# Middle of the mixer in a hybrid encoder layer: meta rows in four column groups, fewer and wider cumulative-sum products among the value products, one activation table set

## What is computed

```python
log_a = log_sigmoid(a1 @ gla_w_a2 + gla_b_a) / TAU          # GLA decay
cum = cumsum(log_a over the chunk); total = cum[last]
k_dec = k * exp(total - cum); u = k_dec^T v; S = exp(total) * S + u; o = q S
dt = softplus(dt_raw + bias); cum = cumsum(dt * a over the chunk)   # SSD, the same form
w = exp(total - cum) * dt; u = B^T (w * xs); h = exp(total) * h + u; y = C h
mix = concat(rms_norm(o) * silu(og), rms_norm((y + d * xs) * silu(z)))
h = layer_norm(alpha * h + mix @ w_out)
h = layer_norm(alpha * h + sum over the 4 experts of gate * (clamped_swiglu(h Wg, h Wu) Wd))
```

## Time and profile before

| | before |
|---|---|
| median of 3 runs | 1094.92 us (1094.44 to 1095.21) |
| the profiled execution | 1093.93 us, of which the span of instructions is 1091.9 us |
| PE busy | 1029.9 us (94%), mean granted clock 0.993 |
| DVE, ACT, POOL busy | 227.2, 145.7, 25.4 us |
| moved by DMA | 426.54 MB, 391 GB/s over the span |
| mixer, to the first expert product | 0 to 176.5 us |

### The profile page before, as it was taken

How to read it: one execution, slowest core, us unless ns; L and a number is a source line. 1 busy time by engine, 2 the same in 40 slices (tenths; PEclk the granted TensorE clock), 3 DMA queues, 4 the chain that set the end, 5 groups by cost and what they waited for, 6 DMA issues and landing times.

```text
span 1091.9 us, 12309 instructions
## 1 busy us (share of the span) xinstructions
PE 1029.9 (94%) x5060; PEld 452.4 (41%) x5060; DVE 227.2 (21%) x496; ACT 145.7 (13%) x345; POOL 25.4 (2%) x47
## 2 busy tenths in 40 slices
PE   9999999999999999999999999999999999999995
PEld 8887745434333443333333333333333333333331
DVE  5422464111111111111111111111111111111114
ACT  2241413111111111111100111111001111101100
POOL 1230100000000000000000000000000000000000
PEclk9989999999999999999999999999999999999998
DMA  9894449999999999999999999999999999999994
GB/s 321 269 349 155 133 161 384 409 431 426 428 427 428 427 428 429 428 428 429 429 428 427 429 429 429 428 427 430 429 428 429 428 429 428 427 429 427 429 427 170
DMA packets 51471, 426.54 MB, mean 391 GB/s; under 512 B 8058, under 2 KB 24547, under 8 KB 26483
## 3 DMA queue, kind: packets, MB, share of 16 engines
q1 hardware_dynamic: 48738, 423.78, 93.4%
q10 hardware_dynamic: 2704, 2.36, 0.8%
HBM read 425.08 MB, written 1.05 MB: 390 GB/s over the span
## 4 chain that ended last, share of the span: by engine, by line
PE 56%; DMA 41%; DVE 2%; ACT 1%; issue 0%; POOL 0%; DVEq 0%; SPq 0%; POOLq 0%
DMA ring<-in_moe_w_up 22%; PE bank L1066 20%; DMA ring<-in_moe_w_gate 18%; PE bank L1105 12%; PE bank L1046 3%; PE bank L1038 3%; PE bank L747 3%; PE bank L944 3%; PE bank L933 1%; PE bank L887 1%; PE bank L703 1%; PE bank L823 1%; PE bank L1094 1%; PE bank L1057 1%; PE bank L763 1%; PE bank L849 1%
## 5 line engine op out<-in xcount | busy, mean ns | idle before, releaser
L1066 PE MATMUL bank<-ring,arena 128*64 128x512 f32 x2000 | 449.0, 595 | 43.9 <-DMA ring<-in_moe_w_up 33.2
L1066 PEld LDWEIGHTS bank<-ring,arena 128*64 128x64 f32 x2000 | 138.1, 136 | 323.9 <-issue 237.9
L1105 PE MATMUL bank<-ring,arena 128*64 128x512 f32 x1024 | 226.8, 595 | 0.7 <-issue 0.7
L1105 PEld LDWEIGHTS bank<-ring,arena 128*64 128x64 f32 x1024 | 71.1, 137 | 151.9 <-issue 151.9
L1470 DVE COPY arena<-bank 128x512 f32<-128x512 f32 x32 | 22.1, 692 | 324.5 <-PE bank L1105 324.5
L656 ACT ACTIVATE arena<-arena 128x512 f32<-128x512 f32 x32 | 20.1, 630 | 457.6 <-DVE arena L1457 457.6
L1046 PE MATMUL bank<-arena 64*128 64x512 f32 x256 | 72.0, 640 | 0.9 <-DVE arena L1470 0.9
L1038 PEld LDWEIGHTS bank<-arena 128*128 128x128 f32 x480 | 58.8, 196 | 22.8 <-issue 22.8
L1463 DVE TENSOR_SCALAR arena<-bank 128x512 f32<-128x512 f32 x32 | 22.1, 691 | 217.8 <-PE bank L1066 217.8
L667 ACT ACTIVATE arena<-bank 128x512 f32<-128x512 f32 x32 | 19.1, 597 | 343.0 <-PE bank L1094 343.0
L1038 PE MATMUL bank<-arena 128*128 128x128 f32 x480 | 64.5, 288 | 0.0
(11 more groups left out here) (271 smaller groups left out, 499.9 us busy)
## 6 DMA issues: line engine op xcount, KB each, us to landing
ring<-in_moe_w_down SPq DMA_DIRECT2D x64, 2048.0 KB, 35.4
ring<-in_moe_w_up SPq DMA_DIRECT2D x63, 2048.0 KB, 34.8
ring<-in_moe_w_gate SPq DMA_DIRECT2D x62, 2048.0 KB, 31.9
ring<-in_w_in SPq DMA_DIRECT2D x12, 1024.0 KB, 12.8
ring<-in_w_out SPq DMA_DIRECT2D x4, 1024.0 KB, 12.2
arena<-in_moe_w_gate SPq DMA_DIRECT2D x4, 1024.0 KB, 7.1
arena<-in_moe_w_up SPq DMA_DIRECT2D x2, 1024.0 KB, 9.1
arena<-in_x SPq DMA_DIRECT2D x2, 512.0 KB, 4.7
```

The source lines that it names most:

```text
L1066: ins = mm(b[h * SL:(h + 1) * SL, :], (xA[pp], xB)[q][:, k, par * SL:(par + 1) * SL], unit_at(UPM * m + q, k)[:, h * 512:(h + 1) * 512], s ...
L1105: ins = mm(bank[6][h * SL:(h + 1) * SL, :], hidT[:, kt % 4, (kt // 4) * SL:(kt // 4 + 1) * SL], unit_at(2 * UPM + q, k)[:, h * 512:(h + 1) ...
```

## The change

`MH` gets four groups of 16 partitions (0, 32, 64, 96) in place of two. Each meta product is cut to half the moving columns and twice the count: keys 64 columns, values 128, logits 64. ACT and DVE handle the four groups as one instruction over 112 partitions, in place of two instructions. In the GLA update of the meta chunk each head now stands on its own row group, with a `link` before each head but the first.

The sums: `dt_m` is `dt_c` masked into four chunk columns by `ind` (a 128x2 indicator of the two halves), made by one more DVE instruction, so that one product with `ones` gives all SSD totals; the triangle product takes both token halves at once. The GLA totals take `la` as the stationary operand of 128 rows and `ind` as two moving columns. Two links go. The keys' second half moves behind the logits, the SSD sums stand between the two halves of the first value products, and the meta triangle products stand each behind a quarter of the second value products; `D_ps` is signalled after the last of these. Products of odd and even chunks alternate in `ssd_update` and `ssd_out`.

On ACT the set `natural_log_exp_and_others` is loaded ahead of the softplus and again behind the Sigmoid of z. The transposes of the SSD half move before the last quarter of the og products, and their copies between the two Sigmoids of og, into a tile `mixY` of its own.

```diff
...
-MH = (slice(0, META), slice(64, 64 + META))
-MH1 = 64 + META
+MH = tuple(slice(32 * g, 32 * g + META) for g in range(4))
+MH1 = 96 + META
 SR = 64 + GRANK + SHEADS
-HK, HV = GKEY // 2, GVAL // 2
+HK, HV = GKEY // 4, GVAL // 4
 RING = 8
...
         la = cut(10368, NT, GKEY)
-        expD = cut(10880, GKEY // 2, parts=MH1)
+        expD = cut(10880, HK, parts=MH1)
         qT = cut(11136, 2, SEQ)
         cacc = cut(11648, 2, TOK)
...
+            nc.scalar.preload_act_table_set("natural_log_exp_and_others")
...
             tmpf = tmp[:, :, :].rearrange("p t n -> p (t n)")
             link(nc.scalar.activation(tmpf, bank[2][:, :], ACT.Abs))
-            for m in MH:
-                link(nc.scalar.activation(expD[m, :], bank[0][m, 0:HK], ACT.Abs))
+            mh = slice(0, MH1)
+            link(nc.scalar.activation(expD[mh, :], bank[0][mh, 0:HK], ACT.Abs))
             link(nc.scalar.activation(tmpf, tmpf, ACT.Exp, scale=-1.0))
-            for m in MH:
-                link(nc.scalar.activation(expD[m, :], expD[m, :], ACT.Exp, scale=-1.0))
+            link(nc.scalar.activation(expD[mh, :], expD[mh, :], ACT.Exp, scale=-1.0))
             link(nc.scalar.activation(tmpf, tmpf, ACT.Ln, bias=1.0))
-            for m in MH:
-                ins = nc.scalar.activation(expD[m, :], expD[m, :], ACT.Ln, bias=1.0)
-            ins.then_inc(la_sp, 1)
+            nc.scalar.activation(expD[mh, :], expD[mh, :], ACT.Ln, bias=1.0).then_inc(la_sp, 1)
             act.wait_ge(dsum_ps, 1)
...
                 nc.scalar.activation(z_t[:, t, :], bank[(0, 5)[t]][:, :], ACT.Sigmoid).then_inc(z_sig, 1)
...
+            act.wait_ge(mixT_ps, 1)
+            mixT_evac(bank[0], mixY, 0)
+            act.wait_ge(mixT_ps, 2)
+            mixT_evac(bank[5], mixY, 2)
             og_sigmoid(1)
-            act.wait_ge(mixT_ps, 1)
-            mixT_evac(bank[0], 4)
-            act.wait_ge(mixT_ps, 2)
-            mixT_evac(bank[5], 6)
             act.wait_ge(mixT_ps, 3)
-            mixT_evac(bank[6], 0)
...
-            def token_major(outs, n):
-
-                for t in range(NT):
-                    for kt in range(KT):
-                        ins = mm(outs[t], hT[:, kt, META + t * P:META + (t + 1) * P], wslot(n, kt), start=kt == 0, stop=kt == KT - 1)
+            def token_major(out, n, t):
+
+                for kt in range(KT):
+                    ins = mm(out, hT[:, kt, META + t * P:META + (t + 1) * P], wslot(n, kt), start=kt == 0, stop=kt == KT - 1)
                 return ins
             def meta_rows(dst, cols, slots):
...
-            token_major([bank[4][:, t * 256:(t + 1) * 256] for t in range(NT)], U_K)
-            meta_rows(bank[1][:, 256:256 + HK], HK, ((U_K, 0), (U_K, HK))).then_inc(k_ps, 1)
+            token_major(bank[4][:, 0:256], U_K, 0)
+            meta_rows(bank[1][:, 64:64 + HK], HK, [(U_K, g * HK) for g in range(4)])
             pe.wait_ge(sT_ok, 1)
             for dst, a, m in ((bank[1][:, 0:8], META, P), (bank[1][:, 8:16], META + P, P), (bank[1][0:META, 16:24], 0, META)):
                 ins = mm(bank[0][m, 0:HK], sT[:, 0:META], w_a2e[:, g * HK:(g + 1) * HK], start=True, stop=True)
             ins.then_inc(la_ps, 1)
+            token_major(bank[4][:, 256:512], U_K, 1).then_inc(k_ps, 1)
+
             pe.wait_ge(w_landed[U_V], 16)
             pe.wait_ge(conv, 8)
             pe.wait_ge(cT_ok, 6)
-            token_major([bank[5][:, 0:256], bank[7][:, 0:256]], U_V)
+            token_major(bank[5][:, 0:256], U_V, 0)
             pe.wait_ge(dt_ok, 1)
-            for t in range(NT):
-                mm(bank[6][:, t * 8:(t + 1) * 8], tri[:, :], dt_c[:, t, :], start=True, stop=True)
+            mm(bank[6][:, 0:16], tri[:, :], dt_c[:, 0:NT, :], start=True, stop=True)
             mm(bank[6][0:META, 16:24], tri[0:META, 0:META], dt_c[0:META, 2, :], start=True, stop=True)
-            for c in (0, 2, 1, 3):
-                r = CHUNK * (c % 2)
-                if c == 1:
-                    link(ins)
-                ins = mm(bank[6][:, 32 + c * 8:40 + c * 8], ones[r:r + CHUNK, :], dt_c[r:r + CHUNK, c // 2, :], start=True, stop=True)
-            ins.then_inc(dsum_ps, 1)
-
+            mm(bank[6][:, 32:64], ones[:, :], dt_m[:, :, :], start=True, stop=True).then_inc(dsum_ps, 1)
+
+            token_major(bank[7][:, 0:256], U_V, 1)
             pe.wait_ge(la_ok, 1)
             for t in range(NT):
                 mm(bank[2][:, t * 256:(t + 1) * 256], tri[:, :], la[:, t, :], start=True, stop=True)
-            mm(bank[0][MH[0], 0:HK], tri[MH[0], MH[0]], la_m[MH[0], :], start=True, stop=True)
-            for c in (0, 2, 1, 3):
-                r = CHUNK * (c % 2)
-                if c == 1:
-                    link(ins)
-                    mm(bank[0][MH[1], 0:HK], tri[MH[1], MH[1]], la_m[MH[1], :], start=True, stop=True)
+            for t in range(NT):
                 for i in range(2):
-                    ins = mm(bank[0][:, GKEY + i * 4 + c:GKEY + i * 4 + c + 1], la[r:r + CHUNK, c // 2, i * P:(i + 1) * P],
-                             ones[r:r + CHUNK, 0:1], start=True, stop=True)
-            ins.then_inc(D_ps, 1)
+                    at = GKEY + i * 4 + 2 * t
+                    mm(bank[0][:, at:at + 2], la[:, t, i * P:(i + 1) * P], ind, start=True, stop=True)
             pe.wait_ge(w_landed[U_V + 1], 16)
-            n = U_V + 1
-            for dst, at in ((bank[5], META), (bank[7], META + P)):
-                for kt in range(KT):
-                    ins = mm(dst[:, 256:512], hT[:, kt, at:at + P], wslot(n, kt), start=kt == 0, stop=kt == KT - 1)
-                ins.then_inc(v_ps, 1)
-            meta_rows(bank[3][:, 0:HV], HV, ((U_V, 0), (U_V + 1, 0))).then_inc(v_ps, 1)
+            for n, (m, dst, at) in enumerate(zip(MH, (bank[5], bank[5], bank[7], bank[7]), (META, META, META + P, META + P))):
+                for kt in range(4 * (n % 2), 4 * (n % 2) + 4):
+                    ins = mm(dst[:, 256:512], hT[:, kt, at:at + P], wslot(U_V + 1, kt), start=kt == 0, stop=kt == KT - 1)
+                if n % 2:
+                    ins.then_inc(v_ps, 1)
+                ins = mm(bank[0][m, 0:HK], tri[m, m], la_m[m, :], start=True, stop=True)
+                if n == 3:
+                    ins.then_inc(D_ps, 1)
+            meta_rows(bank[3][:, 0:HV], HV, [(U_V + g // 2, (g % 2) * HV) for g in range(4)]).then_inc(v_ps, 1)
             pe.wait_ge(wx_ok, 1)
             ssd_banks = (1, 6, 4, 1, 6)
-            def ssd_update(c):
-                b = bank[ssd_banks[c]]
-                for g in range(SGRP):
-                    if c == 0:
-                        k, w = Bt[0:META, 2, g * SST:(g + 1) * SST], xs[0:META, 2, g * 256:(g + 1) * 256]
-                    else:
-                        r = CHUNK * ((c - 1) % 2)
-                        k, w = Bt[r:r + CHUNK, (c - 1) // 2, g * SST:(g + 1) * SST], xs[r:r + CHUNK, (c - 1) // 2, g * 256:(g + 1) * 256]
-                    ins = mm(b[:, g * 256:(g + 1) * 256], k, w, start=True, stop=True)
-                ins.then_inc(us_ps, 1)
+            def ssd_update(c, g):
+                if c == 0:
+                    k, w = Bt[0:META, 2, g * SST:(g + 1) * SST], xs[0:META, 2, g * 256:(g + 1) * 256]
+                else:
+                    r = CHUNK * ((c - 1) % 2)
+                    k, w = Bt[r:r + CHUNK, (c - 1) // 2, g * SST:(g + 1) * SST], xs[r:r + CHUNK, (c - 1) // 2, g * 256:(g + 1) * 256]
+                ins = mm(bank[ssd_banks[c]][:, g * 256:(g + 1) * 256], k, w, start=True, stop=True)
+                if g:
+                    ins.then_inc(us_ps, 1)
             pe.wait_ge(kdec, 1)
-            for c in range(3):
-                ssd_update(c)
+            for g in range(SGRP):
+                ssd_update(0, g)
+            for g in range(SGRP):
+                for c in (1, 2):
+                    ssd_update(c, g)
             pe.wait_ge(w_landed[U_Q], 16)
             pe.wait_ge(v_ok, 1)
             def gla_update(c):
...
+                    if c == 0 and h:
                         link(ins)
                     dst = b[64 * (h % 2):64 * (h % 2) + 64, at + (h // 2) * GDV:at + (h // 2 + 1) * GDV]
                     if c == 0:
-                        m, i = MH[h // 2], h % 2
-                        kk, vv = k_m[m, i * GDK:(i + 1) * GDK], v_m[m, i * GDV:(i + 1) * GDV]
+                        kk, vv = k_m[MH[h], :], v_m[MH[h], :]
                     else:
                         r = CHUNK * ((c - 1) % 2)
                         kk, vv = k_t[r:r + CHUNK, (c - 1) // 2, h * GDK:(h + 1) * GDK], v_t[r:r + CHUNK, (c - 1) // 2, h * GDV:(h + 1) * GDV]
...
                 ins = gla_update(c)
             ins.then_inc(ug_ps, 1)
-            for c in (3, 4):
-                pe.wait_ge(Ss_ok, c - 2 + 0)
-                ssd_update(c)
+            pe.wait_ge(Ss_ok, 2)
+            for g in range(SGRP):
+                for c in (3, 4):
+                    ssd_update(c, g)
             pe.wait_ge(q_ok, 1)
...
-            def ssd_out(c):
```

(36 more changed lines are left out.)

41 lines of the change are left out of this document (21 added, 20 removed).

## The result

The changed kernel takes 1086.32 us (median of 4 runs, 1085.14 to 1087.47), the kernel before 1094.79 (1094.44 to 1095.21). The prediction was wrong in its size; its mechanism held.

The account below looks back on a forecast made before the run. PE's work before the last mixer product sets, one to one, when the saturated weight stream starts. Terms -1.1 - 2.2 - 1.4 - 1.7 + 0 + 0.3 + 0.1 + 1.0 - 0.9 = -5.9 us gave 1089.0, range 1087.0 to 1092.4.

Parts of the forecast that it names:

- Rival D: Stream start: PE time is saved but the stream starts no earlier, loads already issued filling it; 1094.9 us, chance 0.04.
- C: Rival: clock still falls once, at the sums or between meta keys and time steps; costs 3.3, 1092.3 us, chance 0.10.
- E: Rival: clock falls at meta keys with time steps, marked totals and GLA meta update; 3.3 each, 1098.9 us, chance 0.04.
- links: GLA meta update: three links in place of one, two more times 0.5, so 1.0 us worse; the one certain loss.
- alternation: SSD updates and outputs: chunks already run in pairs, so alternating their order gains 0, to 0.3 us better.
- F: Rival: products keep their order on PE, so alternation pairs chunks in SSD updates and outputs; 2.6 us gained, 1086.4, chance 0.05.
- Meta keys: Meta key products on PE: 64 instructions at 29 ns take 1.86 us again, no gain; ends 0.9 better, 1.5 worse.
- B's worst case: Rival: four column groups run no faster than two; with 52 ns for both meta products 1092.0 us; rival's chance 0.15.
- GLA sums: GLA sums on PE: 4.42 us become 2.2, triangles 1.06 and eight two-column products 1.1; gain 2.2 us.
- Second value products: Second value products on PE: 9.77 us become 8.4, 7.1 at full clock plus four meta triangles at 0.32; gain 1.4.
- if a load stayed, 7 us would cover it: ACT's tables before the SSD sums: two wide halves on PE, 7 us, would hide a remaining table load of 1.28 us.
- The change of the chain to the stream: Profile sign: the chain that ended last changes from PE to the stream's transfers at about 393 us, before at 399.

Follow-up runs that it names:

- the pair: The changed kernel with one link in the GLA meta update and the four meta triangles together behind the marked totals: 1083.69 us, ratio 0.9904.
- all three: The changed kernel with one link in the GLA meta update, meta triangles together and GpSimd's long products behind the logarithms: 1083.84 us, ratio 0.9908.

## Why the prediction was wrong in size and right in kind

Right, by its own steps:
- PE's order of work sets the start of the stream, one to one: 7.86 us earlier on PE, 7.8 of span, and 6.4 to 7.0 for 7.1 added in the mixer. Rival D is out.
- No clock fall at the sums (1.00 from 68 to 78), nor there in any other profile with the new sums, so the 3.3 us came back, and C is out. E named a real danger: of its three places the GLA meta update does see falls, in three profiles of kernels with the new sums (transposes put back, GpSimd later, triangles together). That the profiled execution of the changed kernel has none was luck in part.
- Meta values 1.88 (forecast 1.86), links +0.95 (+1.0), transposes -1.05 (-0.9, shown by their undoing), alternation 0 (shown), SSD sums 0.70 (0.8). F is out, although its number, 1086.4, is nearly the one measured: that is chance, since its 2.6 us of pairing are not there.

The step that failed is the size of several terms of PE's sum, 1.9 us in all; the largest is the one for the meta keys, put at nothing:
- Meta keys, the largest: 0 forecast, -0.84 measured. I took 29 ns for one instruction as a floor, since no row showed less. No row showed four column groups with so few columns either. They passed at 16 ns, and at 9 ns with 32 columns. With B's worst case, 52 ns, this was doubt in the wrong direction.
- GLA sums: -2.2 forecast, -2.75 measured. The eight products of two columns on 128 rows took 0.81 us in place of 1.1, and the triangle ahead of them 0.86 in place of 1.06. Both now stand between full-height products, where in before a 16-row product followed; two profiles fit with that. Where products of 64 rows followed (the kernel with old sums) the triangle took 0.96, and where 16-row products followed (triangles together) the eight took 0.88. The range gave all the sums 0.2 us of room, and they came 0.7 better.
- Second value products: -1.4 forecast, -1.25 measured. One spread triangle costs 0.35 (8.52 less 7.11, divided by 4). The form used there was close, but four together cost 0.23 in all: so 1.2 of the 1.4 us is the price of the spreading. That this part of the change loses time against the simple order was nowhere in the forecast; I had set it beside the old 9.77 alone.
- Small ones: SSD sums -0.14, cut halves -0.17 (0.13 for three restarts, not 0.3), wait ahead of the SSD updates -0.1, transposes -0.15, logits -0.1.

A further 0.7 us of the miss in the median comes from the starting point: the profiled execution of before lay 1.0 under its median, that of after 0.3, in runs that scatter by 2.3. This took the time out of the range: with PE's 7.85 us alone it would be 1094.92 - 7.85 = 1087.07, just inside. The range counted only the prices of PE's work and left no room for executions that differ by more than 2 us.

A reason that fell though its number held: "if a load stayed, 7 us would cover it". The tables did bring nothing that the rows show, but the 7 us were not there. The chain of the time steps ended 0.06 us before PE came, held by GpSimd's products, and in executions in which the clock rose earlier at the start (at 5.35 and 6.2 us in place of 8.34) PE waited there 1.17 and 0.38 us (the kernel with chunk order put back, and the changed kernel's second profile). The same holds in all six profiles with GpSimd's products in their place in which the clock rose by 6.2 us: PE waits 0.38 to 1.30 us, and in those with a later rise no wait shows. I had read DVE's durations from an execution in which GpSimd was done, and moved them to a place where it isn't.

The change of the chain to the stream was forecast at about 393 us. It came at 440 in the profile. The chain of before has its next such transfer at 446.56, so the same step of the work is 6.2 us earlier, but the chain now changes over at that one and not at the one before. That view is no good measure of where the stream starts.

```profile
440.32 31.93 DMA ring<-in_moe_w_gate
```

Open: why the clock falls at the GLA meta update in some executions. It did in 4 of 12 profiles with three links and in none of 6 with one (two groups, one link, the pair, all three, and the two of the kernel before), which points to the links but doesn't prove it. The pair's rows give 2.07 us (102.76 in place of 104.83 from the SSD sums to the first expert product), its medians 2.6 to 3.2; falls that it avoids would fit with that, and so would chance between the runs.

## What to carry to other kernels

When a profile shows a saturated stream behind a serial part, add up the serial part's starts, edit by edit: the sum comes out one to one. Give every term of such a sum both ends, and don't take the smallest duration in the trace as a floor for a shape that the trace doesn't hold. Small products of one odd tile shape belong together, and an engine's step that is moved earlier must be priced beside what the neighbour engine does at its new time.
